# Layer two's twelve mid conditioning pieces, moved behind the query weights and into the attention's units

## The reference, cut to what matters

```
sh1, sc1, gt1, sh2, sc2, gt2 = split(silu(c) @ ada_w[layer] + ada_b[layer], 6)
h = modulate(rms_norm(x, norm_g[layer, 0]), sh1, sc1)
y = nsa_attention(h, w_qg, w_o, *shared)           # layer two
x = x + gt1 * rms_norm(y, norm_g[layer, 1])
h = modulate(rms_norm(x, norm_g[layer, 2]), sh2, sc2)
x = x + gt2 * rms_norm(sq_relu_mlp(h, up, down), norm_g[layer, 3])
```

## Time and profile before

| | us |
|---|---|
| median of 3 runs | 1109.18 (1107.68 to 1109.24) |
| the profiled execution | 1113.71, its span 1111.9 |
| busy: TensorE / VectorE / ScalarE / GpSimd | 882.9 / 660.4 / 408.8 / 161.1 |
| chain that ended last: TensorE / VectorE / issue / ScalarE / DMA | 63% / 20% / 6% / 5% / 3% |
| mean granted clock of TensorE | 0.892 |

### The profile page before, as it was taken

The page is one execution under the profiler, slowest core; times in us unless marked ns, Lnnn a source line. Parts: engine busy times, 40 slices in busy tenths (PEclk is TensorE's granted clock), DMA queues, the critical chain, the costliest instruction groups (busy, mean ns, idle before and its releaser), DMA issues.

```text
span 1111.9 us, 17342 instructions
## 1 busy us (share of the span) xinstructions
PE 882.9 (79%) x7433; PEld 768.1 (69%) x7433; DVE 660.4 (59%) x684; ACT 408.8 (37%) x541; POOL 161.1 (14%) x200
## 2 busy tenths in 40 slices
PE   2386897577887764999999947875777949999996
PEld 2255885567776453989998847774445739899984
DVE  5852678466544355899965074757545345755553
ACT  2133541323332226343444073303455253444351
POOL 8611410423432110000000041300000000000000
PEclk9987998699889777999999868976899878999998
DMA  8801432323213124799965238827000135755550
GB/s 337 245 1 38 152 114 79 111 78 116 77 41 116 75 71 157 257 378 371 372 190 191 97 100 290 272 92 298 1 1 1 48 104 190 267 189 189 189 190 38
DMA packets 71805, 170.15 MB, mean 153 GB/s; under 512 B 5401, under 2 KB 6705, under 8 KB 71730
## 3 DMA queue, kind: packets, MB, share of 16 engines
q1 hardware_dynamic: 68784, 160.75, 41.9%
q0 software_dynamic: 2384, 7.15, 2.2%
q10 hardware_dynamic: 562, 1.15, 0.3%
HBM read 166.42 MB, written 1.05 MB: 151 GB/s over the span
## 4 chain that ended last, share of the span: by engine, by line
PE 63%; DVE 20%; issue 6%; ACT 5%; DMA 3%; POOL 2%; ACTq 0%; DVEq 0%; SPq 0%; POOLq 0%
PE ps L1609 7%; PE ps L1611 7%; PE ps L1596 7%; PE ps L1613 7%; PE ps L1598 7%; PE ps L1599 7%; DVE wlo L1008 3%; PE ps L1391 2%; DVE gt L956 2%; DVE acc L956 2%; PE ps L1779 2%; PE ps L1538 2%; PE ps L1424 2%; DMA raw<-in_ada_w_dram 2%; ACT whi L629 1%
## 5 line engine op out<-in xcount | busy, mean ns | idle before, releaser
L1008 DVE TENSOR_TENSOR wlo<-raw,whi 128x2048 fp32r<-128x2048 f32 x94 | 218.6, 2326 | 99.7 <-ACT whi L629 98.2
L629 ACT ACTIVATE whi<-raw 128x2048 fp32r<-128x2048 f32 x94 | 178.6, 1907 | 177.2 <-DMA raw<-in_mlp_down_dram 87.7
L1596 PE MATMUL ps<-ghi,whi 128*128 128x256 f32 x576 | 167.9, 292 | 21.5 <-ACT ghi L825 10.1
L1598 PE MATMUL ps<-glo,whi 128*128 128x256 f32 x576 | 167.2, 290 | 0.0
L1599 PE MATMUL ps<-ghi,wlo 128*128 128x256 f32 x576 | 167.1, 290 | 0.0
L1596 PEld LDWEIGHTS ps<-ghi,whi 128*128 128x128 f32 x576 | 115.2, 200 | 23.4 <-issue 17.6
L1598 PEld LDWEIGHTS ps<-glo,whi 128*128 128x128 f32 x576 | 115.0, 200 | 0.5
L1599 PEld LDWEIGHTS ps<-ghi,wlo 128*128 128x128 f32 x576 | 114.9, 199 | 0.0
L1609 PE MATMUL ps<-whi,hidhi 128*128 128x512 f32 x256 | 101.1, 395 | 0.0
L1611 PE MATMUL ps<-whi,hidlo 128*128 128x512 f32 x256 | 100.5, 393 | 0.0
L1613 PE MATMUL ps<-wlo,hidhi 128*128 128x512 f32 x256 | 100.2, 391 | 0.0
(11 more groups left out here) (329 smaller groups left out, 1735.6 us busy)
## 6 DMA issues: line engine op xcount, KB each, us to landing
raw<-in_ada_w_dram SPq DMA_DIRECT2D x32, 1024.0 KB, 6.9
raw<-in_mlp_up_dram SPq DMA_DIRECT2D x32, 1024.0 KB, 5.6
raw<-in_mlp_down_dram SPq DMA_DIRECT2D x32, 1024.0 KB, 5.1
late<-in_ada_w_dram SPq DMA_DIRECT2D x16, 1024.0 KB, 8.9
late<-in_kv_ada_w_dram SPq DMA_DIRECT2D x8, 1024.0 KB, 8.0
raw<-in_kv_w_dram SPq DMA_DIRECT2D x6, 1024.0 KB, 6.2
raw<-in_rw_k_dram SPq DMA_DIRECT2D x4, 1024.0 KB, 12.6
raw<-in_rw_r_dram SPq DMA_DIRECT2D x4, 1024.0 KB, 5.2
```

The costliest lines, as they stand in the source:

```text
L629: sc.activation(whi[i][:, :, :], raw[i][:, :].rearrange("p (k n) -> p k n", k=4), ACT.Copy).then_inc(s_hi, 1)
L1008: st.tell(dv.tensor_tensor(wlo[i][:, :, :], raw[i][:, :].rearrange("p (k n) -> p k n", k=4), whi[i][:, :, :].bitcast(F32), ALU.subtract), ...
L1596: mm(out_, whi[b][:, k, cols], hi[:, k0 + k, :], start=(first and k == 0 and m % 2 == 0), stop=False, skip_group_check=True)
L1598: mm(out_, whi[b][:, k, cols], lo[:, k0 + k, :], start=False, stop=False, skip_group_check=True)
```

## The change

The stream holds all six kv pieces, then the four query pieces, then the twelve mid pieces, then the four output pieces. VectorE's sums leave the projections. A new function, `ada_half`, issues one half of a piece; units 1 to 12 have two of them each, one between `prob` and `o_copied`, one behind `maxima`. The first output pieces' `weight_high` and `weight_low` move into the last units, and those of piece q0 + 6 stand ahead of the split of the output.

```diff
--- before.py
+++ after.py
@@ -374,9 +374,9 @@
         place_feed_forward(0)
         kv_pieces = [w_piece(A["kv_w"], 512 * kh, 512 * b) for b in range(3) for kh in range(2)]
         mid_pieces = [x for part in (2, 3, 4) for x in ada_pieces(ada1, part)]
-        place("kv", kv_pieces[:2] + [x for n in range(4) for x in (kv_pieces[2 + n], mid_pieces[n])])
-        place("q", [x for n in range(4) for x in (square(A["nsa_wqg"][0])[n], mid_pieces[4 + n])] + mid_pieces[8:])
-        place("wo", square(A["nsa_wo"][0]))
+        place("kv", kv_pieces)
+        place("q", square(A["nsa_wqg"][0]))
+        place("wo", mid_pieces + square(A["nsa_wo"][0]))
         place_feed_forward(1)
         LATE_AFTER = {marks["ff0"] + 2 + a: a for a in range(20)}
         LATE_AFTER.update({marks["ff1"] + 4 + 2 * a: 20 + a for a in range(4)})
@@ -891,8 +891,6 @@
             act.wait_ge(n_hx, 1)
             sc.activation(hx[:, :, :], hx[:, :, :], ACT.Tanh, scale=GELU).then_inc(n_tanh, 1)
             q_half(1)
-            weight_high(q0 + 4)
-            weight_high(q0 + 5)
             def exps(u):
                 j, tb = UNITS[u]
                 keys = P * (tb + 1)
@@ -920,10 +918,11 @@
                     act.wait_ge(n_masks, 2)
                 sc.activation(pcT[0:16, u % 2, :, :].rearrange("p e q -> p (e q)"), ps[0:16, 6, 0:2 * P], ACT.Copy)\
                   .then_inc(n_pcT, 1)
+                if u > 12:
+                    weight_high(q0 + u - 9)
             act.wait_ge(n_o, len(UNITS))
             for h in range(2):
                 sc.activation(half_of(ghi, h), half_of(oT, h), ACT.Copy).then_inc(n_zhi, 1)
-            weight_high(q0 + 6)
             weight_high(q0 + 7)
             post_norm(q0 + 8)
             pre_norm(4, "gmB2", "shB2", ghi, q0 + 8)
@@ -958,6 +957,14 @@
 
             def column(b, n):
                 return ps[:, b, 256 + 8 * n:264 + 8 * n]
+
+            def ada_half(a, dst, i, k):
+
+                if k == 0:
+                    loaded(v, A_AT[a])
+                src, c = raw[A_AT[a] % RING][:, D * k:D * k + D], V["cs"][:, 2 * i + k:2 * i + k + 1]
+                ins = dv.scalar_tensor_tensor(dst[:, :], src, c, dst[:, :], ALU.mult, ALU.add)
+                st.tell(ins, T["ada"]) if k else st.do(ins)
 
             def shift_cols(src, bias, dst):
                 v.wait_ge(s_cols_ps, T["cols"].n + 1)
@@ -1253,14 +1260,13 @@
             kv0, q0 = marks["kv"], marks["q"]
             pre_norm(0, "gmkv", "shkv", ghi, glo, kv0)
             modulated(0, "gmB1", "shB1", qhi, qlo)
-            def mid_piece(n):
+            for q in range(kv0 + 2, q0 + 2):
+                weight_low(q)
+
+            def mid_half(n):
                 if n == 0:
                     v.wait_ge(n_acc5, 16 * 8)
-                ada_piece(ada_marks["kv"] + n, acc_b[n // 4], n % 4, False)
-
-            for n, q in enumerate(range(kv0 + 2, q0 + 2)):
-                weight_low(q)
-                mid_piece(n)
+                ada_half(ada_marks["wo"] + n // 2, acc_b[n // 8], n // 2 % 4, n % 2)
 
             v.wait_ge(n_stk, 16 * 8)
             for i, pos in enumerate((POSK, POSV)):
@@ -1283,9 +1289,7 @@
             st.do(dv.tensor_scalar(both(hx), both(hx), 0.044715, 1.0, ALU.mult, ALU.add))
             st.tell(dv.tensor_tensor(both(hx), both(hx), both(hc), ALU.mult), T["hx"])
             weight_low(q0 + 2)
-            mid_piece(6)
             weight_low(q0 + 3)
-            mid_piece(7)
             v.wait_ge(n_tanh, 1)
             st.do(dv.scalar_tensor_tensor(both(hc), both(hx), 1.0, both(hc), ALU.add, ALU.mult))
             st.tell(dv.tensor_scalar(both(hc), both(hc), 0.5, None, ALU.mult), T["hc"])
@@ -1305,10 +1309,6 @@
                 rows = slice(64 * e, 64 * e + 64)
                 st.do(dv.tensor_copy(kcmp[rows, :, e, 0:NCMP], ps[rows, 2, 0:60].rearrange("p (g n) -> p g n", g=G)))
             st.tell(dv.tensor_copy(vcmp[0:NCMP, :, :].rearrange("p g d -> p (g d)"), ps[0:NCMP, 2, 64:64 + G * 64]), T["c"])
-            for n in range(8, 12):
-                mid_piece(n)
-            weight_low(q0 + 4)
-            weight_low(q0 + 5)
 
             v.wait_ge(n_sc_ps, 1)
             v.wait_ge(n_masks, 2)
@@ -1349,13 +1349,19 @@
                                        cf[:, u, :].rearrange("p (e b) -> p e b", e=2), gates[:, tb, 2 * j:2 * j + 2, 1:3], ALU.mult))
                 p_ = prob[u % 2][:, :, :, :].rearrange("p e b k -> p (e b) k")[:, :, 0:keys]
                 st.tell(dv.tensor_tensor(p_, p_, cf[:, u, :].unsqueeze(2).to_broadcast([P, 4, keys]), ALU.mult), T["pr"])
+                if 0 < u < 13:
+                    mid_half(2 * u - 2)
                 if u:
                     o_copied(u - 1)
                 if u + 2 < len(UNITS):
                     maxima(u + 2)
+                if 0 < u < 13:
+                    mid_half(2 * u - 1)
+                if u > 13:
+                    weight_low(q0 + u - 10)
             o_copied(len(UNITS) - 1)
+            weight_low(q0 + 6)
             split_z(oT, 2)
-            weight_low(q0 + 6)
             weight_low(q0 + 7)
             v.wait_ge(n_nrow, 64)
             gate_row(4, gB[0], nrow_b[0])
```

## The result

The changed kernel takes 1115.35 us in the median (1112.97 to 1119.96, 8 runs), the kernel before 1109.21 (1107.47 to 1112.85, 8 runs). The ratio is 1.0057, 95% interval 1.0036 to 1.0078: slower by some 6 us. The interval excludes no change, but the difference is smaller than the spread of single runs: beside the experiments the kernel before was run 40 times more and took 1100.5 to 1117.2 us. The forecast was 1114.8. The profiled execution of the changed kernel took 1114.49.

What follows compares the result with a forecast made beforehand. Bounds: the ring in the projections, a VectorE-TensorE loop in the units. -25.0 + 15.7 + 0.5 + 14.4 = +5.6 us takes the profiled 1113.71 to 1119.3; 4.5 less for the median gives 1114.8, range 1100 to 1122.

Steps and rivals of the forecast that it cites:

- Part 1: Projections up to unit 0: without mid pieces in ring and sums, unit 0 starts 25.0 us earlier, bounds 21.8 and 29.9.
- Part 2: Units 1 to 12: first halves hide in VectorE's wait for scores, twelve second halves behind maxima cost 15.7 us.
- Part 3: End of the units: moved output weight splits, with a low part ahead of the last scaling, cost 0.5 us, between 0 and 2.3.
- Part 4: TensorE's clock in the units: wider idle stretches make it fall in about each of six pairs, 2.4 each, 14.4 us.
- The clock that holds: Rival, units: TensorE's clock does not fall despite wider idle stretches, so 1100.4, faster; 18%.
- A brief fall behind the wider gap only: Rival, units: the clock falls only behind the wider gap, six times 1.0 to 1.7, say 7 us: 1107; 17%.
- The low clock throughout: Rival, units: the low clock stays for most of the loop, up to 33.7 us instead of 14.4, about 1130; 8%.
- Less gained in the projections: Rival, projections: a copy or `wlo` chain replaces the ring as bound, e.g. 15 us gained instead of 25: 1125; 7%.

Runs made afterwards that it cites:

- run 40: No label of a kernel: the kernel before, unchanged, was run 40 times more beside the experiments: 1100.5 to 1117.2 us.
- e1: The changed kernel with only the first half of each piece, between scaling and output's copy, in units 1 to 12; second halves left out: 1084.54 us.
- e6: The changed kernel without the twelve mid pieces, neither their transfers nor their sums made, the rest as changed: 1084.31 us.
- e2: The changed kernel with only the second half of each piece, behind the maxima, in units 1 to 12; first halves left out: 1115.15 us.
- e4: The changed kernel with small filler matmuls on TensorE behind each output in units 1 to 12, VectorE's work untouched: 1102.46 us.
- e5: The kernel before, unchanged, run for a second trace: 1109.03 us, once.
- e9: Against the changed kernel: every half moved into VectorE's waits in projections and units, output weights' splits moved into late odd units: 1084.78 us.
- e10: e9 with one change, GpSimd's masks made before it waits for the compression's input: 1083.44 us.
- e3: The changed kernel with both halves of a unit between the scaling and the output's copy, nothing left out: 1094.77 us.

## Why the prediction was right

**Part 1, forecast 25.0, measured 24.4.** From TensorE's first matmul on kv0 to unit 0 the kernel before takes 780.72 - 657.59 = 123.1 us, the changed one 750.70 - 651.96 = 98.7. The steps: to `xcmp` 14.5 earlier (forecast 14.7); `xcmp` itself slower by 0.8, which I did not see: it moved beside GpSimd's masks; the product and the gap behind it 2.9 shorter (3.2), with 1.20 us of idleness ahead of the product where I had said under one; q2 and q3 0.9 shorter, since TensorE is at the low clock for 3.4 us at the beginning of q2 and not for 5.3; the compressed part 7.0 (7.1). That the full 15.15 us of removed work would not come back here, since TensorE's scores are late next, was the step that mattered, and it held in each of the changed kernels.

**Part 2, forecast 15.7, measured 15.8.** The first half is free (e1, e6), the second costs its whole length (e2, and in e4 2.64 us in each of six pairs).

**Part 3, forecast 0.5, measured 0.3 to 1.3.** The prediction put the last scaling 1.7 us later and counted only what this delays TensorE's last transposes. Both steps came out. The last pair takes 10.5 us instead of 8.8 in the kernels at full clock, and the last transposes begin 5.07 us behind unit 14's scaling, where the first trace has 4.50 (3.65 in e5, where TensorE's clock was full at that place). Up to the norm behind the output product the delay is larger: from unit 14's scaling it is 38.9 us in both traces of the kernel before and in e9 and e10, 39.2 in e6, and 40.1 to 40.2 in the seven other kernels with a low part ahead of the last scaling. That is inside the bound of 2.3; on the time nothing of it can be seen (e9).

**Part 4, forecast 14.4, measured 13.6.** The idle stretches came out at the widths worked out where the clock was full ahead of them, 2.97 and 2.10 us. With filler work the clock is at 0.96 and 13.6 us are gone. So the mechanism is shown; the closeness of the number is in part luck. The two bounds (0 and 33.7) were far apart, and the value rested on two prices read from rows, 1.7 and 3.2, and on one fall of 2.4 us in each of six pairs. The six pairs lost 0.7 to 3.0 us each, 11.9 together, and the last pair, which the sum did not have, another 1.7. The rule of the Trainium skill that spoke for the clock to hold (TensorE: Matmul & The Clock Gate, "HAM oscillation — how this bites in real kernels") does not describe this loop: from unit 1 to unit 13 no idle stretch ahead of the transposes is longer than 2.98 us, less than the one it names, and the granted clock of the units was 0.82.

**The sum.** -24.4 + 30.7 = +6.3 us by the traces; the medians differ by 6.1. The growth does not hang on where the units are said to end: from unit 0 to the norm behind the output product both traces of the kernel before take 117.1 us and the changed one 147.8. The two profiled executions differ by 0.8 only, since the one of before was 4.5 above its median and the changed one 0.9 below, and e5 shows where: ahead of the stage. Comparing those two alone one would have called the change neutral.

**The rivals.** The clock that holds (1100.4) is what e4 built by hand (1102.5). A brief fall behind the wider gap only (1107) is excluded by the 13.6 us, where it had 7. The low clock throughout (1130) did not come: in every pair the clock is full again for a part of it. Less gained in the projections (1125) is excluded by e6 and by the trace's 24.4 us.

## What to carry to other kernels

Work that is moved into a loop between two engines is free only where its engine waits anyway, and the loop shows that place: here between the scaling and the copy, not behind the maxima, 30 us apart for the same instructions. Where the added work widens TensorE's idle stretches, its granted clock can be a second price nearly as large as the first (13.6 us beside 15.8). Idle stretches in the trace of before, and what followed them, can warn of it, but they give its size only roughly; in e3 the clock fell with more stretches and none of them wider. If a change frees a stage, name what is late next before counting the removed work as gained.

## What the runs showed of the hardware

- TensorE's clock fell in a loop whose idle stretches were 2.97 and 2.10 us, with work between them, and not in six pairs with 1.66 and 0.78. It also fell, in two pairs of six, with three stretches of 0.78, 1.32 and 1.39 us (e3). What decides was not tried.
- Adding 168 small matmuls made the same kernel 12.9 us faster.
- VectorE's 60-column instructions took up to 0.40 us instead of 0.27 while GpSimd built masks, and 0.28 at most without it.
- In two traces the microseconds above the kernel's median come from matmuls that ran at a lower clock than in other traces, and not at the same place. The first trace of the kernel before loses its microseconds in layer one behind the scan. There 48 matmuls (three lines, 16 each) take 16.7 us from the first start to the last end, and 12.2 in e5. The last of the three lines, first in that trace, then in the changed kernel's:

```profile
378.66 7.03 PE L1645 MATMUL ps<-rs,indt 16*128 16x256 f32 x16
```

```profile
375.79 5.11 PE L1651 MATMUL ps<-rs,indt 16*128 16x256 f32 x16
```

e10's profiled execution, 5.9 us above its median, loses them far earlier. The same 32 matmuls in the changed kernel's trace and in e10's:

```profile
79.55 10.10 PE L1430 MATMUL ps<-tg,gb 128*128 128x256 f32 x32
```

```profile
78.97 15.16 PE L1434 MATMUL ps<-tg,gb 128*128 128x256 f32 x32
```

The granted clock there is 1.00 and 0.63, and the stages behind start some 5 us later. What decides between the two was not tried.
